# Two more additions on VectorE, eight fewer column sums on TensorE, at six stage borders

## The reference, cut to what matters

```
def _rms_norm(x, g):
    xf = x.astype(jnp.float32)
    y = xf * lax.rsqrt(jnp.mean(xf * xf, axis=-1, keepdims=True) + EPS)
    return (y * g.astype(jnp.float32)).astype(x.dtype)
...
        hf = _swiglu(_rms_norm(x, g[0]), ffn_w_gate[layer, 0], ffn_w_up[layer, 0], ffn_w_down[layer, 0])
        x = x + 0.5 * _rms_norm(hf, g[1])
        xn = _rms_norm(x, g[2])
```

## Time and profile before

| | us |
|---|---|
| median of 3 runs | 2651.99 (2651.78 to 2655.93) |
| the profiled execution | 2655.2, of which span 2653.5 |
| TensorE busy (matmuls) | 2549.3, 96% of the span |
| GpSimd busy | 1296.8, 49% |
| VectorE busy | 1024.0, 39% |
| ScalarE busy | 986.5, 37% |

### The profile page before, as it was taken

How to read it: one execution, slowest core, us unless ns; L and a number is a source line. 1 busy time by engine, 2 the same in 40 slices (tenths; PEclk the granted TensorE clock), 3 DMA queues, 4 the chain that set the end, 5 groups by cost and what they waited for, 6 DMA issues and landing times.

```text
span 2653.5 us, 31276 instructions
## 1 busy us (share of the span) xinstructions
PE 2549.3 (96%) x11478; PEld 2064.5 (78%) x11478; DVE 1024.0 (39%) x1577; ACT 986.5 (37%) x1333; POOL 1296.8 (49%) x681
## 2 busy tenths in 40 slices
PE   8999999999999999999999999999999998989997
PEld 6888878755888888888888777678888877867676
DVE  3222231055522211522212640635222983724965
ACT  5333323277533333433332333434333423233543
POOL 5555445400455554655544543226555545256863
PEclk9999989989999999899999999888999998999998
DMA  3333432200233333233332222012332444323741
GB/s 135 100 97 100 138 119 87 89 15 1 64 111 95 95 103 103 79 95 96 101 104 95 74 85 88 8 40 94 97 95 95 151 141 152 112 86 87 184 119 64
DMA packets 79993, 251.64 MB, mean 95 GB/s; under 512 B 9731, under 2 KB 14211, under 8 KB 79788
## 3 DMA queue, kind: packets, MB, share of 16 engines
q1 hardware_dynamic: 72384, 235.55, 28.5%
q10 hardware_dynamic: 6684, 11.90, 1.3%
q0 software_dynamic: 848, 3.15, 0.3%
HBM read 237.54 MB, written 15.25 MB: 95 GB/s over the span
## 4 chain that ended last, share of the span: by engine, by line
PE 76%; issue 11%; POOL 7%; DVE 2%; ACT 2%; DMA 1%; SPq 0%; POOLq 0%; DVEq 0%; ACTq 0%
PE banks L1809 20%; PE banks L1810 20%; PE banks L1811 20%; POOL wl_sb L384 6%; PE banks L1882 2%; PE banks L1755 2%; PE banks L1883 2%; PE banks L1887 2%; DMA raw_sb<-weights 1%; PE banks L1763 1%; PE banks L865 1%; PE banks L640 1%; PE banks L874 1%; PE banks L881 1%; PE banks L597 1%
## 5 line engine op out<-in xcount | busy, mean ns | idle before, releaser
L384 POOL TENSOR_TENSOR wl_sb<-raw_sb,wh_sb 128x1024 fp32r<-128x1024 f32 x401 | 975.9, 2437 | 1036.1 <-ACT wh_sb L376 1033.0
L1809 PE MATMUL banks<-xh_sb,wh_sb 128*128 128x512 f32 x2064 | 809.4, 392 | 19.6 <-POOL wl_sb L384 12.3
L1810 PE MATMUL banks<-xh_sb,wl_sb 128*128 128x512 f32 x2064 | 805.9, 390 | 0.0
L1811 PE MATMUL banks<-xl_sb,wh_sb 128*128 128x512 f32 x2064 | 805.6, 390 | 0.0
L376 ACT ACTIVATE wh_sb<-raw_sb 128x1024 fp32r<-128x1024 f32 x401 | 423.9, 1059 | 781.8 <-DMA raw_sb<-weights 734.8
L1809 PEld LDWEIGHTS banks<-xh_sb,wh_sb 128*128 128x128 f32 x2064 | 389.2, 189 | 112.0 <-issue 16.8
L1811 PEld LDWEIGHTS banks<-xl_sb,wh_sb 128*128 128x128 f32 x2064 | 388.9, 188 | 81.6
L1810 PEld LDWEIGHTS banks<-xh_sb,wl_sb 128*128 128x128 f32 x2064 | 389.0, 188 | 80.2 <-issue 0.2
L1809 PE MATMUL banks<-hh_sb,wh_sb 128*128 128x512 f32 x704 | 275.8, 392 | 6.1 <-POOL wl_sb L384 6.1
L1810 PE MATMUL banks<-hh_sb,wl_sb 128*128 128x512 f32 x704 | 275.3, 391 | 0.0
L1811 PE MATMUL banks<-hl_sb,wh_sb 128*128 128x512 f32 x704 | 274.9, 391 | 0.0
(11 more groups left out here) (372 smaller groups left out, 2726.2 us busy)
## 6 DMA issues: line engine op xcount, KB each, us to landing
raw_sb<-weights SPq DMA_DIRECT2D x404, 512.0 KB, 3.5
park<-xs_sb ACTq DMA_DIRECT2D x12, 512.0 KB, 3.5
mix_sb<-scratch SPq DMA_DIRECT2D x16, 258.0 KB, 5.4
hf_sb<-scratch SPq DMA_DIRECT2D x16, 258.0 KB, 5.0
mix_sb<-park SPq DMA_DIRECT2D x4, 1024.0 KB, 7.0
scratch<-scratch ACTq DMA_DIRECT2D x1, 2560.0 KB, 12.2
scratch<-mix_sb SPq DMA_DIRECT2D x8, 259.5 KB, 3.0
x_sb<-x_in SPq DMA_DIRECT2D x8, 256.0 KB, 8.6
```

Of the source, the lines that this page charges most:

```text
L384: pool.tensor_tensor(wl[:, slot, :], raw[:, slot, :], wh_f[:, slot, :], ALU.subtract).then_inc(w_split, 1)
L1809: pe.matmul(dst, wh[:, q, cols], in_hi, start=first, stop=False)
L1810: pe.matmul(dst, wl[:, q, cols], in_hi, start=False, stop=False)
L1811: return pe.matmul(dst, wh[:, q, cols], in_lo, start=False, stop=last)
```

## The change

A semaphore `whole_total` is added. In `post`, behind the last product with x (L2139) and ahead of move(0), VectorE waits for that product and adds the slots SG and SP of piece 7 to `TOTAL[1]` and `TOTAL[2]`, raising `whole_total` with each. In `branch_tensor` the four column sums of `TOTAL[1]` ahead of the spread go; behind the spread, 12 column sums become 8: four of `TOTAL[1]` once `whole_total` has risen by one, four of `TOTAL[2]` once by two. The sums of h squared, ahead of the spread, stay as they are.

```diff
@@ branch_tensor
             col_sum(pe, sums[0], buf[:, TOTAL[0], :], True, False)
             pe.wait_ge(branch_sq, 24 * p + 22)
             col_sum(pe, sums[0], buf[:, S0[1], :], False, True).then_inc(cols_summed, 1)
-            col_sum(pe, sums[1], buf[:, TOTAL[1], :], True, False)
             spread_rate(pe, event, diag_post, 7)
-            col_sum(pe, sums[2], buf[:, TOTAL[2], :], False, False)
-            pe.wait_ge(branch_sq, 24 * p + 23)
-            col_sum(pe, sums[1], buf[:, SG[1], :], False, True)
-            pe.wait_ge(tiles_freed, FREE0 + TILE[name + (".dn" if name.startswith("ffn") else ".out")] + KD)
-            col_sum(pe, sums[2], buf[:, SP[1], :], False, True).then_inc(cols_summed, 1)
+            for w in (1, 2):
+                pe.wait_ge(whole_total, 2 * p + w)
+                mm = col_sum(pe, sums[w], buf[:, TOTAL[w], :], w == 1, True)
+            mm.then_inc(cols_summed, 1)
@@ post
                 scale_x = 8 * p
+                dve.wait_ge(tiles_freed, FREE0 + TILE[section] + KD)
+                for w, slots in ((1, SG), (2, SP)):
+                    dve.wait_ge(acc_ready, ADDED[name] + 16 + w)
+                    total = buf[:, TOTAL[w], :]
+                    dve.tensor_tensor(total, total, buf[:, slots[1], :], ALU.add).then_inc(whole_total, 1)
```

More of the change, by code:

```diff
@@ L244, in build @@
         acc_ready = sem("acc_ready")
+        whole_total = sem("whole_total")
         branch_sq = sem("branch_sq")
```

## The result

| kernel | median us | runs | ratio to before (95% interval) |
|---|---|---|---|
| before | 2652.12 (2645.74 to 2655.93) | 9 | |
| changed | 2662.15 (2655.73 to 2664.26) | 9 | 1.0034 (1.0023 to 1.0045) |
| changed, measured once more on another occasion (e8) | 2659.51 | 6, beside 29 of before at 2651.36 | 1.0033 (1.0020 to 1.0046) |

The changed kernel is slower, by about 9 us (0.0034 x 2652; the interval is 6 to 12). The forecast was 6.3 us slower; the measured median of 2662.15 lies in the range of 2653.5 to 2663.5. The profiled execution of the changed kernel took 2658.72, span 2656.6, which is 3.1 over the profiled span of before.

What follows compares the result with a forecast made beforehand. It took the post tails as bound by TensorE's sums, last by only 0.36 us over VectorE, whose add(0) GpSimd held. Terms 4.5 + 3.4 = 7.9, less 1.6 for the clock, gave +6.3 us: 2658.3, range 2653.5 to 2663.5.

Steps and rivals of the forecast that it cites:

- (a): Six posts, ahead of the spread: removing four column sums frees at most 0.1 us in ffn0, worth 0.
- (b): Behind the spread: eight sums cost 3.31 to 3.41 us, 1.7 less, but must wait for the new additions.
- (c): VectorE ahead of move(0): GpSimd holds up the two additions, delaying copies and x; +4.5 and +3.4, sum 7.9 us.
- The slack of 1.1 behind ffn1 and mlstm: Start of ffn1's next stage: xl_sb ready 1.1 us before its matmul, so 1.9 late costs +0.8; mlstm taken as +0.7.
- the 7.9: Six tails: forecast loss from the additions before the clock term, 4.5 + 3.4 = 7.9 us.
- (d): Restarts ahead of attn, mlstm and even: shorter half-speed stretches after a later restart win back 1.6 us.
- The sums were the path: Rival, tails: column sums bound the posts, additions hidden, so faster, 2646 us; chance 0.04.
- The late x is caught up: Rival, behind the posts: x delay shrinks and the clock is kind; +3 us, 2655, no measurable change; chance 0.18.
- The clock turns against it: Rival, TensorE idle before the sums: three restarts each last 1.2 longer; +11.5 us, 2663.5; chance 0.08.

Runs made afterwards that it cites:

- e8: The changed kernel measured again beside the kernel before, on the same chip; 2659.51 us for 2651.36, ratio 1.0033.
- e2: Changed kernel without the two additions and their waits, 8 column sums left behind the spread, statistics of x incomplete; 2647.71 us, ratio 0.9983.
- e3: Changed kernel with ScalarE's last high part of each post ahead of its last squares, so GpSimd's low part runs before the additions; 2649.24 us, ratio 0.9987.
- e6: e5 plus ScalarE's last high part of each post moved ahead of its last squares, as in e3; 2656.02 us, ratio 1.0022.
- e9: Changed kernel with both additions behind move(0) instead of ahead of it; 2654.83 us for 2650.72, ratio 1.0014.
- e7: Kernel before plus one semaphore that nobody uses; 2653.09 us, ratio 1.0001.
- e11: Kernel before plus 12 one-column memsets at VectorE's start that nobody reads; 2653.2 us, ratio 1.0004.
- e1: Kernel before plus only the two additions, at the change's place, results unread, all 24 column sums kept; 2665.84 us for 2651.51, ratio 1.0053.
- e12: The kernel of e1 measured again: kernel before plus only the two additions, results unread; 2660.52 us for 2650.72, ratio 1.0036.
- e4: Kernel before with ScalarE's last high part of each post moved ahead of its last squares; 2654.35 us, ratio 1.0004.
- e5: Kernel before with only the SG addition, put ahead of the reciprocal; TOTAL[1] summed ahead of the spread, 8 sums behind it; 2646.23 us for 2651.36, ratio 0.9984.

## Why the prediction was right, and where it was off

**(a) Four sums ahead of the spread, worth 0.** Right: the spread starts at 382.13, 0.34 behind the start of the diagonal, as it did in the earlier trace rows (383.08 and 382.74), now with 0.96 idle ahead of it.

**(b) Eight sums cost 3.31 to 3.41.** They took 3.57 in ffn0 and 3.58 in attn, 0.2 more; why isn't shown. The first matmul behind attn came +0.48 later, not +0.35. e2 shows what fewer sums are worth if nothing is put in their place: 4.5 us.

**(c) The additions.** This step carried the forecast, and its mechanism is right in each row: the first addition ends 0.54 behind GpSimd, the copy has no wait before it, and comes +1.50, +1.50 and +1.31 later for +1.58, +1.56 and +1.38. In attn the wait for xl_sb grew from 0.19 to 1.82; in ffn1 there is one of 0.67, in mlstm of 0.46, which gave +1.03 and +1.01 for +0.8 and +0.7. That GpSimd causes it is shown by e3, in which the additions take 1.29, and from the other side by e6 and e9.

The sizes, though, were read from one execution that was slower than the median. The slack of 1.1 behind ffn1 and mlstm came of TensorE's lateness in that execution. In e7 and e11, with the same instructions, TensorE already waits 0.26 to 0.38 for xl_sb there and the blocks end at 28.4 and 28.5, not 29.3. Against them the changed kernel, at 30.3, is 1.8 to 1.9 later in each, as in attn. In the same way the copy of ffn0 comes at 8.42 in e7, so that the change costs 1.9 there and not 1.5. By these traces the 7.9 were too low.

**(d) The clock term of -1.6.** This is the term that should not have stood. The base was the median, 2652.0, but the long half-speed stretches were those of one execution that took 2655.2: its 3.2 over the median hold that excess already. It was taken off twice. The traces bear this out. From the first matmul to the end of the blocks the mean of ffn0, ffn2 and ffn3 is 19.25 in the profiled execution of before, 18.66 and 18.43 in the two of the changed kernel, but also 18.69 in e7 and 18.90 in e11: most of what was won back is between executions, and not of the change. Without the term the sum is 7.9, and with the 0.4 outside the span 8.3; the two measurements give 9.0 and 8.7. Their intervals reach down to 6 and 5, so the times alone don't reject the 6.3; the traces speak against it.

The profiled pair shows how large the clock's part is in a single pair. These are stretches of the changed kernel (PEclk is the third number from the end): from the end of mlstm's first three blocks to its post, and then, in ffn1's start, ahead of a dip of the clock, in it and behind it:

```profile
1488.60:1802.20 313.60, 298.25 (x1352) 235.66 (x1351) 129.33 (x251) 117.70 (x147) 110.71 (x79) 0.95 0.21 66
...
725.00:729.60 4.60, 2.78 (x12) 1.97 (x12) 4.57 (x5) 2.95 (x4) 4.60 (x4) 0.98 0.00 0
729.60:733.00 3.40, 3.40 (x10) 2.64 (x9) 1.05 (x2) 0.00 (x0) 0.77 (x1) 0.53 0.00 0
733.00:737.00 4.00, 4.00 (x24) 3.41 (x23) 1.12 (x2) 0.00 (x0) 0.00 (x0) 1.00 0.37 103
```

and of the kernel before, the same stage:

```profile
1483.30:1801.90 318.60, 303.16 (x1353) 239.39 (x1352) 129.28 (x251) 117.66 (x147) 110.48 (x79) 0.93 0.20 65
```

No instruction of that stage changed, yet it took 5.0 us less, with the clock at 0.95 for 0.93. That hid more than half of the 8.1 of the tails in this pair. In attn's case it went the other way: behind the wait of 1.82 the clock fell to half for a while, and +1.9 became +3.54. In e1, e8 and e12, with 1.70 to 1.82 of wait at the same place, it didn't (30.3 each), so this is a draw that the wait doesn't always bring. The 29 executions of the kernel before that ran beside e1 to e4 lie between spans of 2645.1 and 2660.1, at mean granted clocks from 0.966 to 0.961, the longest spans at the lowest clocks. The difference of two single spans says little here.

**The rivals.** *The sums were the path* had a true core, the 4.5 of e2, but not under these additions. *The late x is caught up* fell: x was late by 1.92 in attn, ffn1 and mlstm alike. *The clock turns against it* can't be shut out as a small part: the mean clock of the changed kernel's 9 runs is 0.9626 and that of 29 of before is 0.9638, and in e8 it is 0.9630 for 0.9642. Against it, the restarts behind the copy didn't grow (18.66 and 18.43 for 18.69 to 19.25, above), and the tails account for the loss.

## What to carry to other kernels

Before work is moved from the busiest engine to one that seems idle, look at who runs beside the new place: here an addition of two SBUF tensors took 2.6 us next to a GpSimd instruction and 0.7 when it stood 2.6 us earlier (e5). The same additions and sums turned from +9 us to -3 when GpSimd's instruction was moved away from them (e3). A slow instruction whose wait is hidden (add(0) before the change, 1.92 for 0.68) is a warning: whatever is put ahead of it takes over its wait. And what is read from one profiled execution, a slack as much as a correction, belongs to that execution's own time, not to the median.

## What the runs showed of the hardware

- A VectorE addition of two SBUF tensors, 0.68 us alone, that meets a running GpSimd subtraction ends 0.54 to 0.55 us behind it, whenever it began (386.92 for 386.38 in the kernel before, 383.11 for 382.56 in e6). In the whole trace of the kernel before, 155 such two-SBUF instructions of VectorE began while a GpSimd subtraction had over 0.1 us to go. None ended ahead of it: 146 ended 0.54 to 0.58 behind it, the other nine 0.02 to 0.04. The one addition of e5 that did end first (1390.54 to 1391.22) began 0.02 after GpSimd's subtraction, and that took 2.94 for 2.35. Instructions with an operand in PSUM pass beside it (0.69 in e9; 0.67 to 0.70 for 214 of 217 in the kernel before). A trace shows the hold as a longer duration and not as idle time.
- Column sums one behind the other don't bring back the granted clock: in the kernel before it is 0.50 over the 24 records of attn, which take 5.12. The changed kernel's 16 records in ffn0 take 3.57 at 0.50. In e2, begun right behind the spread, 16 took 2.05 at a mean clock of 0.86.
- Kernels with both additions have 2.12 to 2.15 us between span and run time, all others 1.74 to 1.76; neither the semaphore (e7) nor 12 further VectorE instructions (e11) make it. Its cause is open.
